# Sliding attention in steps of two heads: stacked queries and keys, and the sink as a column of scores

## What is computed

```python
kb, vb = band(k), band(v)                  # previous and own block of 128 keys
scores = jnp.einsum('bnqgrd,bnkgd->bngrqk', qb, kb) * (SWA_HEAD_DIM ** -0.5)
valid = (dist >= 0) & (dist < WINDOW) & (blk * WINDOW + kj[None] - WINDOW >= 0)
scores = jnp.where(valid[None, :, None, None], scores, -jnp.inf)
sink = sinks.astype(jnp.float32).reshape(1, 1, SWA_KV_HEADS, SWA_GROUP, 1, 1)
m = jnp.maximum(scores.max(axis=-1, keepdims=True), sink)
p = jnp.exp(scores - m)
probs = p / (p.sum(axis=-1, keepdims=True) + jnp.exp(sink - m))
out = jnp.einsum('bngrqk,bnkgd->bnqgrd', probs, vb)
```

## Time and profile before

| | us |
|---|---|
| median of 3 runs | 4131.22 |
| lowest and highest run | 4123.99 and 4135.74 |
| the profiled execution, first to last instruction | 4126.4 |
| PE busy | 3789.4 (92%) |
| PE loading weights | 2959.1 (72%) |
| DVE busy | 1773.6 (43%) |
| ACT busy | 1140.1 (28%) |
| POOL busy | 977.8 (24%) |

### The profile page before, as it was taken

One profiled execution on the slowest core, in us unless ns is written; L12 is line 12 of the kernel. 1 busy time (PEld: TensorE's weight loads), 2 busy tenths in 40 slices (PEclk: granted clock), 3 DMA queues, 4 the chain that ended last, 5 costly groups with the idle time before them and its releaser, 6 DMA issues.

```text
span 4126.4 us, 54228 instructions
## 1 busy us (share of the span) xinstructions
PE 3789.4 (92%) x17149; PEld 2959.1 (72%) x17149; DVE 1773.6 (43%) x2992; ACT 1140.1 (28%) x1952; POOL 977.8 (24%) x842
## 2 busy tenths in 40 slices
PE   7999898899799988889979999997897999998898
PEld 5777677578677766756868876785686887786586
DVE  3342762542534266253352335346525224534643
ACT  3232151132313114213232224223223223422231
POOL 6746726200475673530000000003000000000300
PEclk9999899999899999999989985898899997599799
DMA  6645415133464552422233320220333321032042
GB/s 228 188 128 161 143 53 175 53 113 105 146 190 124 164 158 64 151 77 92 94 111 93 102 62 1 85 91 1 143 93 112 96 88 41 8 101 66 1 163 102
DMA packets 211419, 430.07 MB, mean 104 GB/s; under 512 B 21206, under 2 KB 28785, under 8 KB 204824
## 3 DMA queue, kind: packets, MB, share of 16 engines
q1 hardware_dynamic: 206952, 402.96, 31.2%
q10 hardware_dynamic: 2928, 21.02, 1.2%
q0 software_dynamic: 1344, 3.76, 0.4%
HBM read 406.58 MB, written 24.75 MB: 105 GB/s over the span
## 4 chain that ended last, share of the span: by engine, by line
PE 75%; POOL 9%; DVE 7%; issue 5%; DMA 2%; ACT 1%; POOLq 0%; DVEq 0%; SPq 0%; ACTq 0%
PE bank L642 17%; PE bank L644 17%; PE bank L643 17%; PE bank L677 7%; PE bank L695 5%; POOL macc L1865 5%; POOL mprod L1858 4%; PE bank L686 3%; PE bank L669 2%; DMA stage<-in_w_in 1%; PE bank L665 1%; PE bank L656 1%; DVE late L1720 1%; PE bank L796 1%; DMA wmod<-in_w_mod 1%
## 5 line engine op out<-in xcount | busy, mean ns | idle before, releaser
L642 PE MATMUL bank<-wlo,act_hi 128*128 128x512 f32 (+1 forms) x3968 | 1571.3, 396 | 100.5 <-DVE wlo L1189 52.0
L643 PE MATMUL bank<-whi,act_hi 128*128 128x512 f32 (+1 forms) x3968 | 1551.7, 391 | 0.0
L644 PE MATMUL bank<-whi,act_lo 128*128 128x512 f32 (+1 forms) x3968 | 1550.0, 391 | 0.0
L1189 DVE TENSOR_TENSOR wlo<-stage,whi 128x1024 fp32r<-128x1024 f32 (+1 forms) x496 | 645.1, 1308 | 1338.7 <-ACT whi L943 1335.3
L943 ACT ACTIVATE whi<-stage 128x1024 fp32r<-128x1024 f32 (+1 forms) x496 | 516.1, 1048 | 1628.1 <-DMA stage<-in_w_in 865.4
L642 PEld LDWEIGHTS bank<-wlo,act_hi 128*128 128x128 f32 x3968 | 755.7, 190 | 285.2 <-DVE wlo L1189 64.7
L644 PEld LDWEIGHTS bank<-whi,act_lo 128*128 128x128 f32 x3968 | 755.6, 190 | 156.4
L643 PEld LDWEIGHTS bank<-whi,act_hi 128*128 128x128 f32 x3968 | 756.9, 191 | 148.3
L1858 POOL TENSOR_SCALAR mprod<-wmod,csil 128x512 f32<-128x512 f32 x384 | 366.8, 955 | 806.7 <-DVE Y L1349 309.0
L1900 POOL TENSOR_TENSOR late<-late 128x512 f32<-128x512 f32 x48 | 66.8, 1403 | 2026.3 <-DVE late L1737 2026.3
L1865 POOL TENSOR_TENSOR macc<-macc,mprod 128x512 f32<-128x512 f32 x360 | 512.4, 1423 | 66.0 <-POOL mprod L1858 66.0
(11 more groups left out here) (198 smaller groups left out, 2516.3 us busy)
## 6 DMA issues: line engine op xcount, KB each, us to landing
stage<-in_w_in SPq DMA_DIRECT2D x352, 512.0 KB, 3.8
wmod<-in_w_mod SPq DMA_DIRECT2D x384, 256.0 KB, 2.9
stage<-in_w_out SPq DMA_DIRECT2D x128, 512.0 KB, 3.7
out<-Y ACTq DMA_DIRECT2D x20, 1024.0 KB, 5.0
zone<-out SPq DMA_DIRECT2D x4, 4096.0 KB, 14.6
stage<-in_w_in SPq DMA_DIRECT2D x16, 320.0 KB, 3.3
Y<-in_x SPq DMA_DIRECT2D x4, 1024.0 KB, 9.1
rpb_tiles<-rpb_pad POOLq DMA_DIRECT2D x16, 224.0 KB, 4.4
```

Source lines behind the costliest of these rows:

```text
L642: pe.matmul(out, hi_x, lo_w, start=(k == 0), stop=False)
L643: pe.matmul(out, hi_x, hi_w, start=False, stop=False)
L644: mm = pe.matmul(out, lo_x, hi_w, start=False, stop=(k == KC - 1))
L1189: dve.tensor_tensor(wlo[:, j % RH, :, 0:width], stage[:, j % RS, :, 0:width], whi[:, j % RH, :, 0:width].bitcast(F32), ALU.subtract).then_ ...
```

## The change

The 16 heads become 8 pairs, a head of one key head (lower) and one of the next key head (upper): heads 0 and 4, 1 and 5, and so on. The query evictions of panels 0 and 1 write the heads in that order, so that a pair's 128 query channels are neighbours, as are two key heads' 128 channels. One job of four full transposes turns a pair: the lower head comes to lie on partitions 0 to 63, the upper one on 64 to 127. There are 2 key jobs and 8 query jobs for 4 and 16. All use one bank, and each waits for the eviction of the one before it.

A step i is pair i // 4 and query tile i % 4. PE makes both heads' scores, one in the upper and one in the lower row half of the array, into two banks (two such sets); then the two or four transposes of step i - 2 into a single bank; then the products of step i - 3 into the two halves of one output bank. Signals go once per step. ACT copies a step's turned probabilities in one instruction of up to 512 columns.

The sink is written by DVE into column 256 of each score bank (at the first two query tiles of a pair, once for each of the two sets of banks), next to the scores. The exponential takes it along as one more column, so the row sum holds it; the sink's own exponential on ACT and the addition on DVE are gone. One reciprocal serves both heads. The rest of the diff renumbers the jobs of later stages (the ten jobs fewer) and takes the sliding branch out of the shared functions.

```diff
-DVE_LINKS1, DVE_LINKS2 = 236, 334
+DVE_LINKS1, DVE_LINKS2 = 236, 302
...
+PAIRS = S_H // 2 * TT
...
-        es = sb("es", [P, 4], at=wmod_at + 2400)
+        sums_s = sb("sums_s", [P, 4, 2], at=wmod_at + 2400)
...
+        PAIR_SCORE, PAIR_TURN, PAIR_OUT, PAIR_JOB = [bank[2:4], bank[4:6]], bank[6], [bank[7], bank[1]], bank[0]
...
-        J1, J2 = 46, 39
+        J1, J2 = 46, 29
         job_done = count("job_done", J1, J2)
         job_ev = count("job_ev", J1, J2, credit=2)
-        score_done = count("score_done", UNITS)
-        max_done = count("max_done", UNITS)
-        exp_done = count("exp_done", UNITS, credit=2)
-        turn_done = count("turn_done", UNITS, credit=4)
-        pt_done = count("pt_done", UNITS, credit=2)
-        pv_done = count("pv_done", UNITS, credit=4)
-        fin_done = count("fin_done", UNITS, credit=2)
+        score_done = count("score_done", UNITS, PAIRS)
+        max_done = count("max_done", UNITS, 2 * PAIRS)
+        exp_done = count("exp_done", UNITS, PAIRS, credit=2)
+        turn_done = count("turn_done", UNITS, PAIRS, credit=4)
+        pt_done = count("pt_done", UNITS, PAIRS, credit=2)
+        pv_done = count("pv_done", UNITS, PAIRS, credit=4)
+        fin_done = count("fin_done", UNITS, PAIRS, credit=2)
...
-        qT_s, kT_s = view(ZT, 4, SEQ), view(ZK, S_KV, SEQ)
+        def by_pairs(ap):
+            return ap.rearrange("p (r g d) -> p g r d", r=4, g=2)
         def keys_of(n):
             return [n] if n == 0 else [n - 1, n]
-        def scores_s(h, n):
-            ks = keys_of(n)
-            return [(qT_s[0:S_D, h % 4, tok(n)], kT_s[0:S_D, h // 4, ks[0] * P:(ks[-1] + 1) * P])]
-
-        BR_S = dict(name="S", first=0, heads=S_H, scores=scores_s, y=0, j0=1, blk=1,
-                    v=lambda h, kt: kv_s[:, kt, (S_KV + h // 4) * S_D:(S_KV + h // 4 + 1) * S_D])
-
-        def tiles_of(br, i):
-            return keys_of(i % 4) if br["name"] == "S" else list(range(TT))
-
-        def dv_of(br):
-            return S_D if br["name"] == "S" else HD
-
-        JOBS_SK = [turn_job([kv_s[:, t, g * S_D:(g + 1) * S_D] for t in range(TT)], S_D, kT_s[0:S_D, g, :])
-                   for g in range(S_KV)]
-        JOBS_SQ = [turn_job([q_s[:, t, h * S_D:(h + 1) * S_D] for t in range(TT)], S_D, qT_s[0:S_D, h % 4, :], -S_SC)
-                   for h in range(S_H)]
+        qT_p, kT_p = view(ZT, 4, SEQ), view(ZK, 2, SEQ)
+        probs_p, probsT_p = view(PP, 3, 2, 2 * P + 4), view(PP + 2048, 4, SEQ)
+        SINK = 2 * P
+        J_KT, J_QT = 1, 3
+        def pair_heads(hp):
+            return 8 * (hp // 4) + hp % 4, 8 * (hp // 4) + 4 + hp % 4
+        def turned_pair(n):
+            if n < J_QT:
+                return kv_s, n - J_KT, kT_p[:, n - J_KT, :]
+            return q_s, n - J_QT, qT_p[:, (n - J_QT) % 4, :]
...
-                sp.wait_ge(fin_done.sem, fin_done.at(1, l, UNITS))
+                sp.wait_ge(fin_done.sem, fin_done.at(1, l, PAIRS))
...
+            def pair_job(l, n):
+                x, c, _ = turned_pair(n)
+                pe.wait_ge(job_ev.sem, job_ev.at(1, l, n))
+                apart(pe)
+                for t in range(TT):
+                    mm = pe.transpose(PAIR_JOB[:, tok(t)], x[:, t, tok(c)], ident[:, :])
+                mm.then_inc(job_done.sem, 1)
+            def pair_score(l, i):
+                hp, n = i // 4, i % 4
+                ks = keys_of(n)
+                w = P * len(ks)
+                pe.wait_ge(exp_done.sem, exp_done.at(1, l, i + 1 - 2))
+                for e in range(2):
+                    half = slice(e * S_D, (e + 1) * S_D)
+                    mm = pe.matmul(PAIR_SCORE[i % 2][e][:, SINK - w:SINK], qT_p[half, hp % 4, tok(n)],
+                                   kT_p[half, hp // 4, ks[0] * P:(ks[-1] + 1) * P], start=True, stop=True)
+                mm.then_inc(score_done.sem, 1)
+            def pair_turn(l, i):
+                nk = len(keys_of(i % 4))
+                pe.wait_ge(exp_done.sem, exp_done.at(1, l, i + 1))
+                pe.wait_ge(pt_done.sem, pt_done.at(1, l, i))
+                for e in range(2):
+                    for x in range(nk):
+                        c = SINK - (nk - x) * P
+                        mm = pe.transpose(PAIR_TURN[:, tok(e * nk + x)], probs_p[:, i % 3, e, c:c + P], ident[:, :])
+                mm.then_inc(turn_done.sem, 1)
+            def pair_pv(l, i):
+                ks = keys_of(i % 4)
+                pe.wait_ge(pt_done.sem, pt_done.at(1, l, i + 1))
+                pe.wait_ge(fin_done.sem, fin_done.at(1, l, i + 1 - 2))
+                for e, h in enumerate(pair_heads(i // 4)):
+                    v = (S_KV + h // 4) * S_D
+                    c = e * S_D
+                    for x, kt in enumerate(ks):
+                        mm = pe.matmul(PAIR_OUT[i % 2][:, c:c + S_D], probsT_p[:, i % 4, tok(e * len(ks) + x)], kv_s[:, kt, v:v + S_D],
+                                       start=(x == 0), stop=(x == len(ks) - 1))
+                mm.then_inc(pv_done.sem, 1)
+            def swa(l):
+                for n in range(J_KT, J_QT + 1):
+                    pair_job(l, n)
+                for i in range(PAIRS + 3):
+                    if i % 4 == 0 and i < PAIRS:
+                        hp = i // 4
+                        if hp + 1 < S_H // 2:
+                            pair_job(l, J_QT + hp + 1)
+                        pe.wait_ge(job_ev.sem, job_ev.at(1, l, J_QT + hp + 1))
+                    if i < PAIRS:
+                        pair_score(l, i)
+                    if 2 <= i < PAIRS + 2:
+                        pair_turn(l, i - 2)
+                    if i >= 3:
+                        pair_pv(l, i - 3)
+                pe.wait_ge(fin_done.sem, fin_done.at(1, l, PAIRS))
...
-                attention(1, l, BR_S, next_queries2)
+                swa(l)
...
+            def take_queries(panel_of):
+                def go(l, p):
+                    for t in (0, 2):
+                        act.wait_ge(lin_done.sem, lin_done.at(1, l, p * TT + t + 1))
+                        act.activation(by_pairs(q_s[:, t, panel_of * PW:(panel_of + 1) * PW]),
+                                       LIN[t][:, :].rearrange("p (g r d) -> p g r d", g=2, r=4), ACT.Copy)\
+                           .then_inc(lin_free[t].sem, 1)
...
-                if br["name"] == "S":
-                    act.activation(es[:, u % 4:u % 4 + 1], sinks[:, i // 4:i // 4 + 1], ACT.Exp, bias=nmx[:, u % 4, 1:2],
-                                   scale=-1.0)
...
+            def pair_exp(l, i):
+                w = P * len(keys_of(i % 4))
+                act.wait_ge(turn_done.sem, turn_done.at(1, l, i + 1 - 3))
+                for e in range(2):
+                    act.wait_ge(max_done.sem, max_done.at(1, l, 2 * i + e + 1))
+                    ins = act.activation(probs_p[:, i % 3, e, SINK - w:SINK + 1], PAIR_SCORE[i % 2][e][:, SINK - w:SINK + 1],
+                                         ACT.Exp, bias=nmx[:, i % 4, e:e + 1], scale=-1.0,
+                                         accum_out=sums_s[:, i % 4, e:e + 1])
+                ins.then_inc(exp_done.sem, 1)
+            def pair_turned(l, i):
+                w = 2 * P * len(keys_of(i % 4))
+                act.wait_ge(turn_done.sem, turn_done.at(1, l, i + 1))
+                act.wait_ge(pv_done.sem, pv_done.at(1, l, i + 1 - 4))
+                act.activation(probsT_p[:, i % 4, 0:w], PAIR_TURN[:, 0:w], ACT.Copy).then_inc(pt_done.sem, 1)
+            def swa(l):
+                for i in range(PAIRS + 2):
+                    if i >= 2:
+                        pair_turned(l, i - 2)
+                    if i < PAIRS:
+                        pair_exp(l, i)
...
-                elif br["name"] == "S":
-                    w = P * len(tiles_of(br, i))
-                    apart(dve)
-                    dve.tensor_tensor_reduce(s[:, 0:w], s[:, 0:w], band[:, 2 * P - w:2 * P], 1.0, sinks[:, h:h + 1],
-                                             ALU.add, ALU.min, nm).then_inc(max_done.sem, 1)
...
-                if br["name"] == "S":
-                    total = den[:, u % 4:u % 4 + 1]
-                    dve.tensor_tensor(total, sm[:, u % 4:u % 4 + 1], es[:, u % 4:u % 4 + 1], ALU.add).then_inc(dve_link.next(), 1)
-                    dve.wait_ge(dve_link.sem, dve_link.now(blk, l))
...
+            def pair_job(l, n):
+                _, _, dst = turned_pair(n)
+                dve.wait_ge(job_done.sem, job_done.at(1, l, n + 1))
+                if n < J_QT:
+                    dve.tensor_copy(dst, PAIR_JOB[:, :]).then_inc(job_ev.sem, 1)
+                else:
+                    dve.tensor_scalar(dst, PAIR_JOB[:, :], -S_SC, None, ALU.mult).then_inc(job_ev.sem, 1)
+            def pair_max(l, i):
+                n, w = i % 4, P * len(keys_of(i % 4))
+                dve.wait_ge(score_done.sem, score_done.at(1, l, i + 1))
+                for e, h in enumerate(pair_heads(i // 4)):
+                    s = PAIR_SCORE[i % 2][e]
```

(32 more changed lines are left out.)

83 lines of the change are left out of this document (38 added, 45 removed).

## The result

| | before | after |
|---|---|---|
| median, same chip, us | 4133.48 (4 runs) | 3952.15 (4 runs) |
| lowest and highest run, us | 4123.99 and 4136.1 | 3946.59 and 3964.73 |
| span of the profiled execution, us | 4126.4 | 3944.8 |
| its mean granted clock | 0.920 | 0.955 |

The ratio is 0.9565, with a 95% interval of 0.9544 to 0.9586: faster by 181 us, where 158 were forecast.

A forecast was written before the change was run, and what follows sets the result against it. PE at half clock bounded the old loop, DVE the new at 2.37 us a step. Stage 4.3 + 75.8 + 1.5 + 2 = 83.6; saved 77.8, 77.5 and 3, together 158.3; 4126.4 - 158.3 + 4.8 = 3973 us, range 3948 to 4058.

The forecast's parts named there:

- the jump of the clock: Sliding attention loops: filled score rows, no half-width job transposes and denser work raise 1.2 to 2.4 GHz within first steps; 0.62.
- The rule weighed in the prediction: Sliding loop: transposes don't count as busy PE for the clock; over a third of PE's time, so half clock, 4049 us.
- PE at full clock: New loop, scores, transposes, products and job of a pair: 8.0 us per four steps, 2.0 a step.
- VectorE, the mis-sized term: New loop, VectorE's evictions, sink copies, maxima, reciprocals, products: 8.67 us per four steps, 2.17 a step, the bound at full clock.
- The wait of 0.2 us a step: New loop at full clock: VectorE waiting for PE, added to 2.17, giving 2.37 a step, 75.8 us for 32.
- The start: Ahead of the loop: three jobs in one bank, each awaiting the last eviction, 1.44 us each, 4.3 us at full clock.
- Filling, emptying and the slow first steps: Each layer's loop: 1.5 us to fill and empty the pipeline, 2 us for a few first steps at half clock.
- The panel behind: Panel after each sliding stage: 3.0 us at clock 0.50 become full clock, saving 1.5 us, 3 for two layers.
- Half clock (B): Rival, new loops: clock stays 0.50 and PE is the bound, 14.3 us per four steps; 4049 us, chance 0.15.
- halves that don't overlap (C): Rival, pair scores: second head adds 0.86 or 0.43, 3.0 us per pair at half clock; 4097 us, chance 0.06.
- The signs that I had named: New loops: clock near 1.00, steps 2.2 to 2.6 us, DVE over 85% busy, paired scores starting together; start over 5 refutes.

The follow-up runs named there:

- pad_rows: The kernel before, with zeros (written by VectorE) below the 64 rows of keys and queries, so each score uses all 128 rows: 3966.57 us.
- kick: The kernel before, with useless full-array matmuls, six ahead of each sliding loop and three in each of its first eight steps: 4022.54 us.
- sink_alone: The kernel before, one head a step, with only the sink written as a score column, executed once: 4060.43 us.
- sink_again: The kernel of sink_alone, executed six times more: 4122.68, 4125.57, 4053.4, 4122.4, 4128.39 and 4122.85 us.
- apart: The changed kernel, with the second head's score issued behind the transposes, so the array's halves work in turn: 4130.57 us.
- pad_sink: The kernel before, one head a step, with zero rows (written by GpSimd) below keys and queries and the sink as score column: 3957.47 us median, ratio 0.9608.

## Why the prediction was right

- **What bounded the kernel before, and the jump of the clock.** Right. The forecast named filled rows as what would let the clock rise, from rows alone, and pad_rows shows it with no other change in the loop. The half-width job transposes, which it named beside them, are still there in pad_rows and did not matter. Its reason in the other direction, that half-filled work lets the clock fall, was too strong: kick held 1.00 with half-filled scores, as the first layer of sink_alone did. The first theory that one takes from the page, that PE was full and so there was too much work, would have given 4049.
- **The rule weighed in the prediction.** In "TensorE: Matmul & The Clock Gate", Part 4, the Trainium skill has it that transposes do not count as a busy PE. Of the new loop's 7.80 us, 2.56 are transposes (three blocks of four, one of two, and the job), and the loop is at 1.00; that case's time, 4049, did not come. Part 1 of the same page says that the throttled state is the default and that activity releases it. That agrees, but here being busy was not enough of it: sink_again shows PE busy 145.00 of 145.00 us at 0.50, and the first layer of sink_alone shows the same steps at 1.00.
- **PE at full clock.** Forecast 8.0 us for a pair's four steps, measured 7.80. The scores, for which no row existed, cost 0.63 and 0.42 against 0.63 and 0.45; the products 0.84 against 0.89.
- **VectorE, the mis-sized term, and the wrong bound at full clock.** Forecast 8.67 us for four steps, and with it the bound; measured 42.8 us busy in 49.3, that is 6.8 for four steps. The order of time on VectorE shows why, in a step with two sink copies (start, length, line, operation):

```profile
2475.05 0.16 DVE L1659 COPY bank<-sinks 128x1 f32<-128x1 f32 x1
2475.21 0.49 DVE L1661 CUSTOM_DVE_ANT_0 bank<-bank,band,sinks 128x256 f32<-128x256 f32 x1
2475.62 0.14 DVE L1661 DVE_READ_ACCUMULATOR2_ANT nmx<- 128x1 f32 x1
2475.62 0.21 DVE L1659 COPY bank<-sinks 128x1 f32<-128x1 f32 x1
2475.68 0.48 DVE L1661 CUSTOM_DVE_ANT_0 bank<-bank,band,sinks 128x256 f32<-128x256 f32 x1
2476.09 0.14 DVE L1661 DVE_READ_ACCUMULATOR2_ANT nmx<- 128x1 f32 x1
```

  I had added maximum and accumulator read, 0.41 + 0.14 for each. The next instruction starts beside the read, so in a row of several only the last read counts, and the second copy costs 0.06 and not 0.164. From 2475.05 to 2476.23 it is 1.18 us for what I had priced at 1.43. Without copies two maxima come to 0.41 + 0.41 + 0.14 = 0.96 against 1.10. The maxima on 128 keys are 0.35 long instead of 0.49, and I had priced all eight alike. Two gate products in a row show as 0.48 us, where I had 2 x 0.283. Lengths of single instructions were summed where their starts should have been subtracted.
- **The wait of 0.2 us a step** that I put on top, for VectorE standing still for PE, has no place where PE is the bound. Together: 75.8 us forecast for 32 steps, 8 x 7.80 - 0.44 = 62.0 measured.
- **The start.** Forecast 4.3 us from three jobs; measured 5.8 and 6.4. There are four: the query job of the second pair stands in the program ahead of the first score (the fourth L798 above), and four turns of 1.44 us are 5.8. I had the waits' mechanism and missed one turn of it. The same slip is in the reading of before, whose 5.3 and 4.5 us hold six jobs (24 transposes) and not five.
- **Filling, emptying and the slow first steps.** Forecast 1.5 + 2; the loop's 67.1 less 62.0 leaves 5.1. A stage thus: -13.8 + 1.5 + 1.6 = -10.7 us against the 83.6 forecast, which is the 72.9 measured. Twice that is most of the 23 us between the saving forecast, 158, and the one measured, 181.
- **The panel behind** the loop, at full clock: right, 1.00. I took the first layer's 3.0 us at 0.50 for both; the second had 5.8, so the term is 4.3 us and not 3.
- **The rivals.** Half clock (B) did not occur in after in any of its 13 executions, all within 3942.8 and 3970.85. For halves that don't overlap (C) I gave 4097, and apart measured 4130.57. Two prices were too low: the second head's score is a full 1.15, where I took the 0.86 of its two passes' difference, and eight products are 1.90, where I took 1.59. The latter stood in B as well. Had the clock stayed low, four steps would have been 19.68 less one set of scores (3 x 1.15 + 0.72), 15.5 us instead of 14.3, and the time some 20 us above the 4049 I gave, an estimate that no run here tried; it would have been outside my range.
- **The signs that I had named.** The clock near 1.00 and VectorE busy over 85% (42.8 of 49.3 us, 87%) came, and the two heads' scores overlap: 0.63 us for both, as long as one head's in kick. A step of 1.95 us is under the 2.2 to 2.6 that I had named, PE's matmuls wait for nobody, and a start of 5.8 and 6.4 us is over the 5 that I had called a sign of a wrong sum. So the bound that I gave for the new loop failed, and the time still came out inside the range, 4 us above its lower end. That is in part luck: this end was made of no waits, no slow start and scatter, and not of a cheaper VectorE, and four of the 13 executions lie below it.

## What to carry to other kernels

When PE is the bound, busy all the time and at granted clock 0.5, look first at how much of the array its instructions fill; zeros in the idle rows were a test of a few lines, worth 166 of 181 us here, before any restructuring. Look then at the pauses just ahead of such a loop and in its first steps, since the state that the clock takes there can last for all of it. And price chains of short instructions by differences of their starts, not by sums of their lengths.

## What was not expected of the hardware

- One and the same loop has two lasting states, 9.84 us for four steps and, in kick, 5.44, and chance can pick: the program of sink_again took 4053.4 and 4128.39 us on the same chip, and even the kernel before once took 4062.74. A single comparison of such a kernel can show 70 us that no edit brought.
- Rows filled with zeros raise the clock as rows with data do (1.00 through the loop of pad_rows).
- At full clock too, a score over 128 rows and the transposes behind it take less time than with a score over 64 rows: the score on 256 keys 0.49 us against 0.63, that on 128 keys 0.22 against 0.42, and two transposes behind it 0.22 against 0.37. What makes the difference wasn't tried; the chains of pad_sink and kick are shown above.
